# A hybrid two-block kernel on one core: last fill tiles split around the joins, root means by square root, meta values in four column groups

## The reference, cut to what matters

```python
def rms_norm(x, g, eps=NORM_EPS):
    y = xf * lax.rsqrt(jnp.mean(xf * xf, axis=-1, keepdims=True) + eps)
...
        mix = jnp.concatenate([y_gdn, y_mla, y_rwkv], axis=-1)
        mix = mix * jax.nn.silu(cols['gate'])
        x = x + mix @ w_out[layer]
    return rms_norm(x, final_norm_g)
```

```python
        y_conv = conformer_branch(glu_a, glu_b, z_conv, ...)
        y_rec = hgrn2_branch(q, f, i, g_rec, ...)
        merged = sigmoid(m_conv) * y_conv + sigmoid(m_rec) * y_rec
        h_res = h_res + merged @ w_out[l]
    return rmsnorm(h_res[:, N_META:], final_g)
```

## Time and profile before

| what | us |
|---|---|
| runs | 3999.26, 3999.64, 4071.46 (median 3999.64) |
| the profiled execution, its own time | 4051.07 |
| its span | 4049.3 |
| TensorE busy (mean granted clock 0.941) | 3696.3 |
| VectorE busy | 2239.2 |
| ScalarE busy | 1343.5 |
| GpSimd busy | 282.1 |

### The profile page before, as it was taken

One profiled execution on the slowest core, in us unless ns is written; L12 is line 12 of the kernel. 1 busy time (PEld: TensorE's weight loads), 2 busy tenths in 40 slices (PEclk: granted clock), 3 DMA queues, 4 the chain that ended last, 5 costly groups with the idle time before them and its releaser, 6 DMA issues. The chain is left out here.

```text
span 4049.3 us, 60119 instructions
## 1 busy us (share of the span) xinstructions
PE 3696.3 (91%) x24904; PEld 2314.2 (57%) x24904; DVE 2239.2 (55%) x3909; ACT 1343.5 (33%) x2281; POOL 282.1 (7%) x233
## 2 busy tenths in 40 slices
PE   7789988979989969998897998799999998999998
PEld 4477545765644457844676664466666666444443
DVE  3475367746653466256774664346666667443453
ACT  3243354324543234145333455412222222131003
POOL 0010000000000011010000000012222222000000
PEclk9899999979999989698998998899999999999999
DMA  4223212120042242211212003211111110312331
GB/s 156 94 81 102 74 37 78 60 76 34 15 145 106 78 117 76 95 33 35 74 60 103 11 9 144 76 32 43 43 42 43 43 37 16 125 57 71 103 110 44
DMA packets 301630, 281.12 MB, mean 69 GB/s; under 512 B 17824, under 2 KB 273952, under 8 KB 301360
## 3 DMA queue, kind: packets, MB, share of 16 engines
q1 hardware_dynamic: 301360, 277.29, 21.2%
HBM read 203.91 MB, written 73.33 MB: 68 GB/s over the span
## 5 line engine op out<-in xcount | busy, mean ns | idle before, releaser
L3332 DVE SCALAR_TENSOR_TENSOR cv<-glu,params,cv 128x1024 f32<-128x1024 f32 x240 | 360.7, 1503 | 6.4
L1451 PE MATMUL ps<-hT,w_cols 128*128 128x512 f32 x576 | 252.9, 598 | 13.6 <-PEq L158 13.6
L399 PE MATMUL ps<-hT,w_cols 128*128 128x512 f32 x448 | 204.1, 616 | 3.2 <-PEq L158 3.2
L1451 PEld LDWEIGHTS ps<-hT,w_cols 128*128 128x128 f32 x576 | 110.3, 192 | 151.3 <-issue 149.4
L3627 PE MATMUL ps<-hT,wr 128*128 128x512 f32 x360 | 161.7, 592 | 0.0
L399 PEld LDWEIGHTS ps<-hT,w_cols 128*128 128x128 f32 x448 | 88.0, 198 | 116.5 <-issue 116.5
L3125 PE MATMUL ps<-w_i,hT 128*128 128x128 f32 x1152 | 135.0, 277 | 0.6 <-DVE glu L3435 0.6
L3125 PEld LDWEIGHTS ps<-w_i,hT 128*128 128x128 f32 x1152 | 130.4, 192 | 1.7 <-DVE glu L3435 0.8
L3308 POOL TENSOR_TENSOR Sp<-Sp,Rp 128x520 f32<-128x520 f32 (+1 forms) x56 | 88.4, 1579 | 574.1 <-DVE W L3349 574.1
L3109 PE MATMUL ps<-hT,w_f 128*128 128x347 f32 x384 | 116.7, 464 | 7.2 <-DMA w_f<-in_w_in 7.2
L3627 PEld LDWEIGHTS ps<-hT,wr 128*128 128x128 f32 x360 | 68.4, 190 | 86.1 <-issue 86.1
(11 more groups left out here) (914 smaller groups left out, 7587.2 us busy)
## 6 DMA issues: line engine op xcount, KB each, us to landing
w_cols<-in_w_in SPq DMA_DIRECT2D x32, 512.0 KB, 3.9
wr<-in_w_in SPq DMA_DIRECT2D x24, 512.0 KB, 5.1
hT_hbm<-hT SPq DMA_DIRECT2D x2, 4096.0 KB, 14.2
hT<-hT_hbm SPq DMA_DIRECT2D x2, 4096.0 KB, 13.7
fh<-hT_hbm SPq DMA_DIRECT2D x16, 512.0 KB, 4.7
fh_again<-hT_hbm SPq DMA_DIRECT2D x16, 512.0 KB, 4.7
x<-in_x SPq DMA_DIRECT2D x8, 512.0 KB, 8.7
ahead<-kb_hbm SPq DMA_DIRECT2D x16, 256.0 KB, 3.4
```

What stands on the lines that cost most here:

```text
L399: q = pe.matmul(ps[:, proj_bank(n, b), :], lhsT=wc[:, n % 3, k, :], rhs=hT[:, k, P + b * 512:P + (b + 1) * 512], start=(k == 0), stop=(k = ...
L1451: q = pe.matmul(ps[:, proj_bank(n, b), :], lhsT=wc[:, n % 3, k, :], rhs=hT[:, k, P + b * 512:P + (b + 1) * 512], start=(k == 0), stop=(k = ...
L3332: vec.scalar_tensor_tensor(out=cv[:, h % 2, :], in0=src, scalar=w, in1=cv[:, h % 2, :], op0=ALU.mult, op1=ALU.add).then_inc(*VEC(f"tap{h}_ ...
```

## The change

Three edits.

1. In `rw_chunk` and `gdn_chunk` only seven of the eight fill tiles are computed ahead of each join. The eighth is computed in two halves of four products each, one between the two sets of 32x32 products of the join and one behind them; in RWKV it goes to bank 6 (`WB`). ScalarE copies it after `right_side` of the half's first step, and TensorE's `first_half` of that step (RWKV) waits for this copy.
2. In `out` and `tail` the factors come from Sqrt on ScalarE and a reciprocal on VectorE in place of Ln and Exp (the diff shows `x_rs`; `g_rs`, `r_rs`, `m_rs` and the tail's `rs` are treated alike).
3. In `hg` token tile 0 is no longer computed whole. Its last 32 columns are multiplied in four groups of output partitions (k modulo 4) into bank 5, ScalarE copies this to `parts`, and one product with `fours` (four 32x32 identities below each other) adds the groups up into the last 32 rows of bank 0. The value tile's other rows are cleared once.

```diff
@@ rw_chunk @@
-                    TURNS += [f"late{n}" for n in range(NT)] + ["pc0_0", "pc0_1", "of0_0", "of0_1"]
+                    TURNS += [f"late{n}" for n in range(NT - 1)] + ["pc0_0", "pc0_1", "of0_0", "of0_1"]
...
+ def last_tile(b, k0, k1):
+     name, h, w = (("late", late_h[1], late_w), ("fill", fh[:, 1], fw))[b]
+     if k0 == 0:
+         pe.wait_ge(*DMA.upto("late_h1" if b == 0 else "fh1", NT // 2))
+         if b:
+             pe.wait_ge(*ACT["w2_3"])
+             pe.wait_ge(*VEC["w2_3"])
+     for k in range(k0, k1):
+         q = pe.matmul(ps[:, WB, 0:REST], lhsT=h[:, k, :], rhs=w[:, k, :], start=(k == 0), stop=(k == KD - 1))
+     if k1 == KD:
+         q.then_inc(*PE(f"{name}{NT - 1}"))
...
  def first_half(s):
+     if s % 4 == 0:
+         pe.wait_ge(*ACT[f"{'fill' if s else 'late'}{NT - 1}"])
...
  def join(b):
      ...
+     last_tile(b, 0, KD // 2)
      pe.wait_ge(*VEC[f"RY{b}"])
      ...
+     last_tile(b, KD // 2, KD)
...
- for n in range(NT):
+ for n in range(NT - 1):
      late_columns(n)
  join(0)
  for s in range(4):
      right_side(s)
+     if s == 0:
+         late_columns(NT - 1)
@@ gdn_chunk @@
- def fill(n):
+ def fill(n, k0=0, k1=KD):
...
+ fill(NT * b + NT - 1, 0, KD // 2)
...
+ fill(NT * b + NT - 1, KD // 2, KD)
...
      right_side(s)
+     if s == 4:
+         filled(2 * NT - 1)
@@ out @@
- act.activation(g_rs, g_ss, FN.Ln, bias=cst("eps"), scale=1.0 / GD)
- act.activation(r_rs, r_ss, FN.Ln, bias=cst("rw_eps"), scale=1.0 / RD)
- act.activation(g_rs, g_rs, FN.Exp, scale=-0.5)
- act.activation(r_rs, r_rs, FN.Exp, scale=-0.5)
+ act.activation(g_rs, g_ss, FN.Sqrt, bias=cst("eps"), scale=1.0 / GD)
+ act.activation(r_rs, r_ss, FN.Sqrt, bias=cst("rw_eps"), scale=1.0 / RD)
...
- act.activation(x_rs[:, r, t:t + 1], x_ss[:, r, t:t + 1], FN.Ln, bias=cst("eps"), scale=1.0 / DM)
- act.activation(x_rs[:, r, t:t + 1], x_rs[:, r, t:t + 1], FN.Exp, scale=-0.5)
+ act.activation(x_rs[:, r, t:t + 1], x_ss[:, r, t:t + 1], FN.Sqrt, bias=cst("eps"), scale=1.0 / DM)
...
+ vec.reciprocal(x_rs[:, r, t:t + 1], x_rs[:, r, t:t + 1]).then_inc(*VEC(f"rs{r}_{t}"))
+ vec.wait_ge(*VEC[f"rs{r}_{t}"])
...
@@ hg @@
  def values(h, b):
-     for t in range(3 * b, 3 * b + 3):
+     for t in range(max(3 * b, 1), 3 * b + 3):
...
+ def meta_values(h):
+     pe.wait_ge(*DMA.upto("w_i", h + 1))
+     for k in range(KD):
+         j = k % 4
+         q = pe.matmul(ps[32 * j:32 * j + 32, BANK_W, 0:P], lhsT=hT[:, k, LAST], rhs=wt["i"][:, k, :], start=(k < 4), stop=(k >= 4))
+     q.then_inc(*PE(f"parts{h}"))
+
+ def meta_sum(h):
+     if h == 0:
+         pe.wait_ge(*DMA["fours"])
+     pe.wait_ge(*ACT[f"parts{h}"])
+     pe.matmul(ps[LAST, BANK_X, 0:P], lhsT=fours[:, :], rhs=parts[:, :], start=True, stop=True)
...
  pe.wait_ge(*VEC[f"glu{h}"])
+ meta_values(h)
  values(h, 0)
  pairs(h, 2)
  values(h, 1)
+ meta_sum(h)
  pairs(h, 3)
...
+ act.wait_ge(*PE[f"parts{h}"])
+ act.copy(parts[:, :], ps[:, BANK_W, 0:P]).then_inc(*ACT(f"parts{h}"))
  act.wait_ge(*PE[f"i{h}"])
...
- act.copy(v[:, :].rearrange("p (b n) -> p b n", b=3), ps[:, BANK_X:BANK_X + 3, 0:3 * P]).then_inc(*ACT(f"v{h}"))
+ act.copy(v[LAST, 0:P], ps[LAST, BANK_X, 0:P])
+ act.copy(v[:, P:3 * P], ps[:, BANK_X, P:3 * P])
+ act.copy(v[:, 3 * P:T2].rearrange("p (b n) -> p b n", b=2), ps[:, BANK_X + 1:BANK_X + 3, 0:3 * P]).then_inc(*ACT(f"v{h}"))
```

More of the change, by code:

```diff
@@ L1089, in late_columns @@
                                     act.wait_ge(*DMA.upto(f"fo{n % 2}", n // 2))
-                                act.copy(fo[:, n % 2, :], ps[:, pair_of_banks(f"late{n}"), 0:TM_LATE]).then_inc(*ACT(f"late{n}"))
+                                act.copy(fo[:, n % 2, :], ps[:, pair_of_banks(f"late{n}") if n < NT - 1 else WB, 0:TM_LATE]).then_inc(*ACT(f"late{n}"))
                             def filled(n):
@@ L1094, in filled @@
                                 act.wait_ge(*DMA.upto(f"fo{n % 2}", NT // 2 + n // 2))
-                                act.copy(fo[:, n % 2, :], ps[:, pair_of_banks(f"fill{n}"), 0:REST]).then_inc(*ACT(f"fill{n}"))
+                                act.copy(fo[:, n % 2, :], ps[:, pair_of_banks(f"fill{n}") if n < NT - 1 else WB, 0:REST]).then_inc(*ACT(f"fill{n}"))
                             def right_side(s):
@@ L1861, in _ @@
                                 pairs(s + 4, 1, 3)
-                            for n in range(NT, 2 * NT):
+                            for n in range(NT, 2 * NT - 1):
                                 fill(n)
@@ L2789, in inverse_norm @@
                             act.wait_ge(*ACT[f"sum{r}_{t}"])
-                            act.activation(x_rs[:, r, t:t + 1], x_ss[:, r, t:t + 1], FN.Ln, bias=cst("eps"), scale=1.0 / DM).then_inc(*ACT(f"ln{r}_{t}"))
-                            act.wait_ge(*ACT[f"ln{r}_{t}"])
-                            act.activation(x_rs[:, r, t:t + 1], x_rs[:, r, t:t + 1], FN.Exp, scale=-0.5).then_inc(*ACT(f"rs{r}_{t}"))
+                            act.activation(x_rs[:, r, t:t + 1], x_ss[:, r, t:t + 1], FN.Sqrt, bias=cst("eps"), scale=1.0 / DM).then_inc(*ACT(f"root{r}_{t}"))
                         def norms(t):
@@ L2802, in meta_norm @@
                             act.wait_ge(*ACT["sum_m"])
-                            act.activation(m_rs[:, :], m_ss[:, :], FN.Ln, bias=cst("eps"), scale=1.0 / DM).then_inc(*ACT("ln_m"))
-                            act.wait_ge(*ACT["ln_m"])
-                            act.activation(m_rs[:, :], m_rs[:, :], FN.Exp, scale=-0.5).then_inc(*ACT("rs_m"))
+                            act.activation(m_rs[:, :], m_ss[:, :], FN.Sqrt, bias=cst("eps"), scale=1.0 / DM).then_inc(*ACT("root_m"))
                         turned(0)
@@ L3013, in build @@
             kS = sbuf(st, "kS", [P, SEQ])
+            fours = sbuf(st, "fours", [P, 32])
+            parts = sbuf(st, "parts_of_meta", [P, P])
             at = sbuf(st, "attn", [P, NT, P])
@@ L3083, in _ @@
                         sp.dma_start(up[block_of(j), OWN, :], io["consts"][block_of(j), at_i:at_i + 32]).then_inc(*DMA("up"))
+                    for j in range(4):
+                        at_i = C_AT["ident"][0] + 32 * j
+                        sp.dma_start(fours[32 * j:32 * j + 32, :], io["consts"][32 * j:32 * j + 32, at_i:at_i + 32]).then_inc(*DMA("fours"))
                     for h in range(KD):
@@ L3739, in norm @@
                         act.wait_ge(*ACT[f"ss{t}"])
-                        act.activation(rs[:, t:t + 1], ss[:, t:t + 1], FN.Ln, bias=cst("eps"), scale=1.0 / DM).then_inc(*ACT(f"lr{t}"))
-                        act.wait_ge(*ACT[f"lr{t}"])
-                        act.activation(rs[:, t:t + 1], rs[:, t:t + 1], FN.Exp, scale=-0.5).then_inc(*ACT(f"rs{t}"))
+                        act.activation(rs[:, t:t + 1], ss[:, t:t + 1], FN.Sqrt, bias=cst("eps"), scale=1.0 / DM).then_inc(*ACT(f"root{t}"))
                 for r in range(2):
@@ L3886, in final @@
                 def final(t):
-                    vec.wait_ge(*ACT[f"rs{t}"])
+                    vec.wait_ge(*ACT[f"root{t}"])
+                    vec.reciprocal(rs[:, t:t + 1], rs[:, t:t + 1]).then_inc(*VEC(f"rs{t}"))
+                    vec.wait_ge(*VEC[f"rs{t}"])
                     vec.scalar_tensor_tensor(out=xt[:, t, :], in0=xt[:, t, :], scalar=rs[:, t:t + 1], in1=fg, op0=ALU.mult,
```

59 lines of the change are left out of this document (35 added, 24 removed).

## The result

| | kernel before | changed kernel |
|---|---|---|
| median | 4042.43 us of 12 runs | 3975.89 us of 12 runs |
| lowest and highest | 3999.26, 4071.46 | 3965.02, 3991.28 |
| profiled execution | 4051.07 | 3983.26 |

The changed kernel is faster: ratio 0.9869, 95% interval 0.9844 to 0.9895, 53 us (42 to 63) of 4042. (The medians lie 66.5 us apart; the ratio is made without the slowest executions, for the kernel before three of twelve, and so shows less.) The forecast was 58.2 us less, but from 3999.6, so 3941: the amount is inside the interval, and the time is 35 us too low.

A forecast was written before the change was run, and what follows sets the result against it. TensorE, busy 91% of the span, was taken as the bound, with its waits and half clock. Savings of 7.4 + 26.2 + 24.6 = 58.2 us off a 3999.6 median gave 3941, range 3905 to 3985.

The forecast's parts named there:

- 1, meta values: Recurrence: four overlapping column groups take 0.69 us plus 0.23 for the sum product, in place of 1.85; 7.4 us saved.
- 2, RWKV: RWKV joins: 1.2 us gained at each by starting at once, plus 9.6 from full clock behind them.
- 2, GDN: GDN joins: 2.6 us gained at each first and 0.5 at each second, plus 5.6 from the clock behind.
- 3, norms: Output stages and tail: two table loads and the Exp go, 2.5 us less a norm; 24.6 us in all.
- so I subtract from the median: 3999.6 - 58.2: Whole kernel: the three-run median is the start, as no term comes from the profiled execution's 28 us stretch; gives 3941.
- rival D: RWKV's last steps: the median too holds a stretch like the 28 us, a warm join avoids it; 3913, chance 0.12.
- this counts on the half tile covering the 3.96 us: First GDN join: half tile covers the wait between groups of 32x32 products, state products at 674.2, not 676.85; gain 2.6.
- Rival E: GDN: idle over 3 us ahead of joins drops the clock through sixteen steps, 7.1 us each; 4055, chance 0.07.
- dense products between and behind: RWKV joins: dense products among the small ones keep full clock, as in the recurrence at 0.98; 9.6 us taken whole.
- Rival C: Meta values in the recurrence: the four column groups do not overlap; 3950, chance 0.06.
- rival B: Norms: Square or Copy is not in Sqrt's set and is loaded again each time, no gain; 3966, chance 0.06.

The follow-up runs named there:

- Experiment 4: Kernel before, unchanged, profiled in four more executions: 4054.81, 4088.26, 4005.07 and 4045.74 us.
- the two undo-experiments: Kernel before with the RWKV part of the fill edit alone, 4006.89 us; changed kernel with the RWKV stage as before, 4011.99 us.
- experiment 5: gdn_early with four products spread through each GDN join, 3964.56 us; gdn_undone with the 1.5 MB weight load after the first state products, 3961.16 us.
- experiment 6: Changed kernel with RWKV's eighth tile whole, between the two sets in each stage's first half, behind both in the second: 3980.75 us.
- before_warm: Kernel before with extra groups of unused products in the last four GDN steps: 4019.28 us, ratio 0.9972.
- gdn_undone: Changed kernel with the GDN stage as before, eight whole fill tiles ahead of each join: 3963.18 us, ratio 0.9837.
- gdn_early: Changed kernel with GDN's first half tile ahead of the wait for the transposes, the second between the two sets: 3950.39 us, ratio 0.9814.

## Why the prediction was right and wrong

| part | forecast | by taking it back | by the stages of the two profiles |
|---|---|---|---|
| 1, meta values | 7.4 | 11.3 | 10.1 |
| 2, RWKV | 14.4 | 36.1 | 41.5 |
| 2, GDN | 11.8 | -12.7 | -8.6 |
| 3, norms | 24.6 | 19.3 | 22.7 and 3.4 at the end |
| sum | 58.2 | 54.0 | 69.1, less 1.3 in the gaps between stages |

The sum was near by luck: two misses of part 2, +21.7 and -24.5, cancelled. (The second is the less certain: by the mean of the stages GDN cost 2 us and not 12.7, and the miss would be some 14.)

**The step that failed first: "so I subtract from the median: 3999.6 - 58.2".** It was 42.8 us off. The kernel before takes 4042.4 in the median of 12 runs. I had seen the stretch of 28 us, called the execution that held it 51 us slow, and taken two short executions for the rule. Experiment 4 shows the opposite: of five profiled executions four hold 54 us of such excess or more. The condition of rival D ("the median too holds a stretch", 0.12) was the case, but its price went off the same median, down to 3913, and a kernel whose median holds a stretch starts at 4042. RWKV's term is the 14.4 that I had plus, on the mean of those five, 35.1 - 5 = 30 us of stretches (5 being the falls behind the second joins that the 14.4 contain); the two undo-experiments give 20 and 36 in all.

**The second: GDN, "this counts on the half tile covering the 3.96 us".** The sum took four pieces of 2.7 us from the first 32x32 product to the state products, 10.8, and put the hole at nothing. The first join took 15.14. The half tile did not cover the hole: it shortened 3.96 to 1.46 us, and 1.00 to 1.40 in the other joins, because what TensorE waits for is its next packet of instructions (experiment 5). And the clock, which the sum has full inside the join, was at half twice: behind the idle of 3.28 us, for 0.5 us lost, since most of it fell on small products, which take 2.9 us at either clock; and behind the hole, for 1.7 us lost in the second half tile. Hole and half clock are 3.7 of the 4.3 us; the rest is that the pieces take 2.85 to 3.05 us at full clock and not 2.7. I had asked only what the idle does to the steps behind; there it did no harm, the state products ran at full clock.

In layer 0 the phases changed like this (profile before to after): up to the first join -1.9, first join +3.2, first step behind it -3.2; fill tiles -2.0, second join +5.1; so 1.1 us lost, and 2.3 in layer 1 by the same phases. To this comes what the last steps make of the clock (+6.3 and -1.1), which differs from execution to execution. Rival E (the idle lets the clock fall and it stays low through the steps, 4055) was right that it falls, and wrong in the rest: it was back before the steps.

**RWKV join: right in size.** Forecast 7.2 us a layer, measured 7.4 in layer 0. The joins took 7.7 to 8.1 us where 7.2 was forecast, all at full clock, and the steps behind gained a little more than forecast. The reason given ("dense products between and behind") was half right: experiment 6 shows that those between do it. What they change is the hole: in the 28 RWKV joins of the seven profiles without the split, a hole of 0.8 to 1.8 us marked "issue" stands in the second set (once, in `before_warm`, just behind it), and low clock starts during each or soon behind it; with the split, or the whole tile between the sets, there is no such hole, and the join and the step behind run at full clock. That the hole and not the density of the work is the cause was not tested by itself.

**Part 1: right in mechanism.** The 16 instructions took 0.65 us against 0.69 in the sum. The sum product hides among the scores, which take 0.87 us with it and 0.69 without, so 0.18 in place of 0.23. With 0.57 from the first of the small products to the next line that is 1.85 - 0.75 = 1.1 us a head, 8.8 in all; the stage gave 10.1, and 13.1 in the profiles of `gdn_undone` and `gdn_early` (811.2 us), of which the longer gap in front of the tail takes 2.3 back. The Trainium skill (TensorE: Matmul & The Clock Gate, Part 3) makes the overlap of weight loads depend on differing row groups; all groups here use all rows, and 0.65 us for 16 instructions, against 1.85 for as many of the full width, speaks against it. Rival C is out.

**Part 3: right, and somewhat high.** One norm has lost 2.5 us as forecast, Square and Copy follow Sqrt without a load (rival B is out), layer 0 gave 3.7 of 3.9, layer 1 19.0 of 17.5. The last gate came 8.9 us earlier in its stage in place of 9.8 (2516.23 and 2470.65 less the stages' starts, 2438.08 and 2401.37), and the wait for it shrank to 5.10, not to nothing: TensorE came earlier too. The undo gives 19.3, less than the stages' 26; the two medians are of different sessions.

## What to carry to other kernels

Before a few per cent are forecast, look at how the kernel's executions differ, stage by stage: a median of three hid 43 us here, and the trace had shown the stretch that explains it. When an edit moves work off an engine ahead of a wait, ask what the idle does to the work directly behind the wait, not only to the stage. A hole that no wait explains has a cause all the same: find what ends it before counting on other work to cover it. And an idle of a microsecond may be worth a few products whose result nobody reads, if half clock behind it costs ten.

## What the runs showed of the hardware

**The clock falls in work with small holes.** GDN's last steps stand still for 2.0 us in a step of 17 at full clock (0.91 and 1.10, above), and they ran at mean clocks from 0.72 to 0.95 in the executions shown. With 0.9 us of extra products in each step the mean was 0.97 and 1.00, and the steps took 66.5 and 64.9 us. The Trainium skill (TensorE: Matmul & The Clock Gate, Part 1) has the clock fall behind idle time, and tells of a kernel where short, frequent idles between groups of products made it fall and rise; the trace agrees with the second too, in steps with no idle longer than 1.1 us. And once RWKV's steps are at half clock they can stay there: steps of 21.7 us in place of 12.2, three in a row, on the same instructions (the kernel before, layer 1, and three more of the ten such places in experiment 4).

**Small products lose nothing at half clock.** The 192 instructions for 32x32 products of one set of a GDN join took 2.91 and 2.94 us where the clock was low for most or all of them (changed kernel, from 655.38 and 792.66), and 2.90 at full clock (`gdn_early`). Products of 384 columns do lose: 8 instructions took 4.54 us in place of 2.85 with the clock at 0.62 in the mean.

**TensorE can run out of instructions.** One set of a GDN join, 192 instructions for products and as many for weight loads, passes in 2.9 us. Its instructions come in packets of 16384 bytes, 256 instructions; in the 11 us of such a join two of them come, and TensorE stands 1.6 and 1.7 us with "issue" as the reason, until 1.4 us after each has landed. With 1.5 MB of weights under way beside them the holes are 4.0 and 2.0 us. Four long products spread between the sets close the holes (joins of 9.1 to 9.5 us, none idle).
